# Feed-forward of a two-layer hybrid backbone: the down products of two inner blocks gather in PSUM before they are added to the running sum

## What is computed

```python
def swiglu(h, w1, w2):
    gate, up = jnp.split(h @ w1, 2, axis=-1)
    return (jax.nn.silu(gate) * up) @ w2
```

## Time and profile before

| | us |
|---|---|
| median of 3 runs | 4626.42 |
| lowest, highest | 4623.34, 4635.23 |
| the profiled execution | 4631.18 |
| its span | 4629.5 |
| TensorE busy with matmuls | 3859.6 (83%) |
| TensorE busy with weight loads | 3059.9 (66%) |
| VectorE busy | 2037.8 (44%) |
| ScalarE busy | 1087.3 (23%) |
| GpSimd busy | 492.6 (11%) |

### The profile page before, as it was taken

One profiled execution on the slowest core, in us unless ns is written; L12 is line 12 of the kernel. 1 busy time (PEld: TensorE's weight loads), 2 busy tenths in 40 slices (PEclk: granted clock), 3 DMA queues, 4 the chain that ended last, 5 costly groups with the idle time before them and its releaser, 6 DMA issues. The chain is left out here.

```text
span 4629.5 us, 55289 instructions
## 1 busy us (share of the span) xinstructions
PE 3859.6 (83%) x22802; PEld 3059.9 (66%) x22802; DVE 2037.8 (44%) x2175; ACT 1087.3 (23%) x1434; POOL 492.6 (11%) x314
## 2 busy tenths in 40 slices
PE   3998468939785999999996899469767859999996
PEld 2887336438674888888884788345356647777774
DVE  3111657645423343444345121667656234544445
ACT  1000332425314111111114000332345131111113
POOL 1000403002005000000003000511022040000000
PEclk6999679968897999999997999679889879999998
DMA  5222430041223101111105222240132211111111
GB/s 185 82 82 79 156 134 21 12 108 23 86 77 123 42 27 41 41 35 32 41 18 164 80 82 78 104 141 5 46 82 68 66 63 51 41 54 41 51 35 73
DMA packets 339917, 320.39 MB, mean 69 GB/s; under 512 B 42718, under 2 KB 310602, under 8 KB 339786
## 3 DMA queue, kind: packets, MB, share of 16 engines
q1 hardware_dynamic: 297514, 265.07, 18.5%
q0 software_dynamic: 6912, 31.46, 2.3%
q10 hardware_dynamic: 35360, 22.02, 1.5%
HBM read 248.17 MB, written 73.30 MB: 69 GB/s over the span
## 5 line engine op out<-in xcount | busy, mean ns | idle before, releaser
L477 PE MATMUL psum<-h_hi,f_whi 128*128 128x512 f32 (+1 forms) x1760 | 485.1, 373 | 70.7 <-DVE f_wlo L922 70.7
L927 DVE TENSOR_TENSOR y<-y,psum 128x1280 f32<-128x1280 f32 (+1 forms) x352 | 476.8, 1355 | 109.3 <-PE psum L477 103.9
L477 PE MATMUL psum<-h_lo,f_whi 128*128 128x512 f32 (+1 forms) x1760 | 481.6, 371 | 0.0
L477 PE MATMUL psum<-h_hi,f_wlo 128*128 128x512 f32 (+1 forms) x1760 | 481.4, 371 | 0.0
L477 PE MATMUL psum<-h_hi,w_hi 128*128 128x512 f32 x1472 | 379.2, 364 | 118.2 <-DVE w_lo L543 118.2
L477 PEld LDWEIGHTS psum<-h_hi,f_whi 128*128 128x128 f32 x1760 | 306.8, 188 | 135.0 <-DVE f_wlo L922 71.2
L477 PE MATMUL psum<-h_lo,w_hi 128*128 128x512 f32 x1472 | 377.4, 363 | 0.0
L477 PE MATMUL psum<-h_hi,w_lo 128*128 128x512 f32 x1472 | 377.0, 362 | 0.0
L922 DVE TENSOR_TENSOR f_wlo<-f_raw,f_whi 128x1024 fp32r<-128x1024 f32 x132 | 161.0, 1221 | 481.9 <-ACT f_whi L893 423.5
L477 PEld LDWEIGHTS psum<-h_hi,w_hi 128*128 128x128 f32 x1472 | 249.9, 190 | 164.3 <-issue 119.1
L893 ACT CAST f_whi<-f_raw 128x1024 fp32r<-128x1024 f32 x132 | 138.4, 1048 | 907.3 <-PE psum L477 882.5
(11 more groups left out here) (264 smaller groups left out, 5706.9 us busy)
## 6 DMA issues: line engine op xcount, KB each, us to landing
f_raw<-in_w_ffn_in SPq DMA_DIRECT2D x88, 512.0 KB, 6.0
proj_cm<-lin_stage POOLq DMA_DIRECT2D x48, 640.0 KB, 4.1
w_raw<-in_w_in SPq DMA_DIRECT2D x48, 512.0 KB, 5.0
ada_w<-in_w_ada SPq DMA_DIRECT2D x24, 1024.0 KB, 10.8
f_raw<-in_w_ffn_out SPq DMA_DIRECT2D x44, 512.0 KB, 3.6
ln_x<-x_cm SPq DMA_DIRECT2D x18, 1024.0 KB, 7.9
att_raw<-proj_cm SPq DMA_DIRECT2D x48, 320.0 KB, 5.7
x_cm<-ln_x SPq DMA_DIRECT2D x14, 1024.0 KB, 4.4
```

Source lines behind the costliest of these rows:

```text
L477: ins = nc.tensor.matmul(out[:, t0:t0 + tn], w, h[:, t0:t0 + tn], start=start and n == 0, stop=stop and n == 2)
L927: nc.vector.tensor_tensor(y[:, o, 0:tokens], y[:, o, 0:tokens], sets(o), ALU.add).then_inc(s_acc.h, 1)
```

## The change

Blocks j = 2p and 2p + 1 form pair p (HP = 11 pairs). The down product is made once per pair: for each of the eight outputs the matmuls of both blocks follow one another into the same PSUM set as one sum, and VectorE adds that to `y` once. The first pair's outputs are copied to `y` instead, and the memset on GpSimd is gone. The down weights of both blocks have to be there at once, so hi and lo of them get buffers of their own, `d_hi` and `d_lo`, two each. Outputs begin in set b. TensorE's order for a pair is gate product of 2p, down product of pair p - 1, up product of 2p, gate and up product of 2p + 1.

```diff
-        w_hi = k.sb(st, "f_whi", [P, 3, D], F32R)
-        w_lo = k.sb(st, "f_wlo", [P, 3, D], F32R)
+        w_hi = k.sb(st, "f_whi", [P, 2, D], F32R)
+        w_lo = k.sb(st, "f_wlo", [P, 2, D], F32R)
+        d_hi = k.sb(st, "f_dhi", [P, 2, D], F32R)
+        d_lo = k.sb(st, "f_dlo", [P, 2, D], F32R)
...
-            @block.gpsimd
-            def _(pool):
-                for j in range(KB):
-                    nc.gpsimd.memset(y[:, j, 0:tokens], 0.0).then_inc(k.sem("y_zero").h, 1)
...
                     act.wait_ge(s_h.h, s_h.at(1) + j)
-                    if not (isinstance(j, int) and j < 2):
-                        act.wait_ge(s_out.h, s_out.at(-KB) + j * KB)
+                    if not first:
+                        act.wait_ge(s_out.h, s_out.at(0) + p * KB)
                     nc.scalar.copy(u_hi[:, q, 0:tokens], hid[:, 0:tokens]).then_inc(s_uhi.h, 1)
-                    hi(2, j, first)
+                    act.wait_ge(s_w[2].h, s_w[2].at(16) + j * 16)
+                    nc.scalar.copy(d_hi[:, q], raw[:, 2]).then_inc(s_hi[2].h, 1)
...
-                def gather(j):
+                def gather(p, first=False):
                     for o in range(KB):
-                        dve.wait_ge(s_out.h, s_out.at(1 + o) + j * KB)
-                        nc.vector.tensor_tensor(y[:, o, 0:tokens], y[:, o, 0:tokens], sets(o), ALU.add).then_inc(s_acc.h, 1)
-
-                def block_j(j, q, more=True):
+                        dve.wait_ge(s_out.h, s_out.at(1 + o) + p * KB)
+                        if first:
+                            nc.vector.tensor_copy(y[:, o, 0:tokens], sets(o + 1)).then_inc(s_acc.h, 1)
+                        else:
+                            nc.vector.tensor_tensor(y[:, o, 0:tokens], y[:, o, 0:tokens], sets(o + 1), ALU.add).then_inc(s_acc.h, 1)
+
+                def block_j(j, q, before=None, first=False, more=True):
                     if more:
                         lo(0, j + 1)
+                    if before:
+                        before()
                     dve.wait_ge(s_silu.h, s_silu.at(1) + j)
...
                     nc.vector.tensor_tensor(hid[:, 0:tokens], act_g[:, 0:tokens], sets(1), ALU.mult).then_inc(s_h.h, 1)
-                    if not (isinstance(j, int) and j < 1):
-                        gather(j - 1)
...
-                dve.wait_ge(k.sem("y_zero").h, k.sem("y_zero").at(KB))
...
-                with dve.Fori(1, HB // 2 - 1) as i:
-                    for q in range(2):
-                        block_j(i * 2 + q, q)
-                block_j(HB - 2, 0)
+                block_j(2, 0, before=lambda: gather(0, True))
+                block_j(3, 1)
+                with dve.Fori(2, HP - 1) as p:
+                    block_j(p * 2, 0, before=lambda: gather(p - 1))
+                    block_j(p * 2 + 1, 1)
+                block_j(HB - 2, 0, before=lambda: gather(HP - 2))
                 block_j(HB - 1, 1, more=False)
-                gather(HB - 1)
+                gather(HP - 1)
...
-                def down(j, q, last=False):
-                    pe.wait_ge(s_lo[2].h, s_lo[2].at(1) + j)
-                    pe.wait_ge(s_ulo.h, s_ulo.at(1) + j)
+                def down(p, last=False):
+                    pe.wait_ge(s_lo[2].h, s_lo[2].at(2) + p * 2)
+                    pe.wait_ge(s_ulo.h, s_ulo.at(2) + p * 2)
                     for o in range(KB):
-                        if o == 0 and not last:
-                            pe.wait_ge(s_silu.h, s_silu.at(2) + j)
-                        elif o == 1 and not last:
-                            pe.wait_ge(s_h.h, s_h.at(2) + j)
+                        if o == 0:
+                            pe.wait_ge(s_h.h, s_h.at(2) + p * 2)
+                        elif o == 1:
+                            pe.wait_ge(s_silu.h, s_silu.at(2 if last else 3) + p * 2)
                         else:
-                            pe.wait_ge(s_acc.h, s_acc.at(o - 1) + j * KB)
+                            pe.wait_ge(s_acc.h, s_acc.at(o - 1) + p * KB)
                         cols = slice(o * P, (o + 1) * P)
-                        ins = three_products(nc, sets(o), chunks, w_hi[:, 2, cols], w_lo[:, 2, cols], u_hi[:, q], u_lo[:, q], True, True)
+                        for q in range(2):
+                            ins = three_products(nc, sets(o + 1), chunks, d_hi[:, q, cols], d_lo[:, q, cols], u_hi[:, q], u_lo[:, q], q == 0, q == 1)
                         ins.then_inc(s_out.h, 1)
...
+                def pair(p, first=False):
+                    if not first:
+                        pe.wait_ge(s_silu.h, s_silu.at(0) + p * 2)
+                    up(0, p * 2)
+                    if not first:
+                        down(p - 1)
+                        pe.wait_ge(s_acc.h, s_acc.at(-1) + p * KB)
+                    up(1, p * 2)
+                    if first:
+                        pe.wait_ge(s_silu.h, s_silu.at(1))
+                    else:
+                        pe.wait_ge(s_acc.h, s_acc.at(0) + p * KB)
+                    up(0, p * 2 + 1)
+                    pe.wait_ge(s_h.h, s_h.at(1) + p * 2)
+                    up(1, p * 2 + 1)
```

More of the change, by code:

```diff
@@ L844, in swiglu @@
     chunks = token_chunks(tokens)
+    HP = HB // 2
     w1 = k.a["w_ffn_in"][l].rearrange("(j p) n -> p j n", p=P)
@@ L858, in swiglu @@
         s_lo = [k.sem(f"{x}_lo") for x in kinds]
-        s_mm = [k.sem(f"{x}_products") for x in kinds]
+        s_mm = [k.sem(f"{x}_products") for x in kinds[:2]]
         s_silu, s_h, s_uhi, s_ulo, s_acc, s_out = (k.sem(x) for x in ("silu_done", "hidden_done", "hidden_hi", "hidden_lo", "acc_done", "down_out"))
@@ L888, in hi, with block_j @@
                     act.wait_ge(s_w[n].h, s_w[n].at(16) + j * 16)
-                    if not first and n < 2:
+                    if not first:
                         act.wait_ge(s_mm[n].h, s_mm[n].at(0) + j)
-                    elif not first:
-                        act.wait_ge(s_out.h, s_out.at(0) + j * KB)
                     nc.scalar.copy(w_hi[:, n], raw[:, n]).then_inc(s_hi[n].h, 1)
-                def block_j(j, q, first=False, more=True):
+                def block_j(j, p, q, first=False, more=True):
                     act.wait_ge(s_mm[0].h, s_mm[0].at(1) + j)
-                    if not first:
+                    if not (first and q == 0):
                         act.wait_ge(s_h.h, s_h.at(0) + j)
@@ L977, in down @@
                         ins.then_inc(s_out.h, 1)
-                def block_j(j, q):
-                    if isinstance(j, int) and j == 1:
-                        pe.wait_ge(s_silu.h, s_silu.at(1))
-                    if not (isinstance(j, int) and j < 2):
-                        pe.wait_ge(s_acc.h, s_acc.at(-2 * KB + KB - 1) + j * KB)
-                    up(0, j)
-                    if isinstance(j, int) and j == 1:
-                        pe.wait_ge(s_h.h, s_h.at(1))
-                    if not (isinstance(j, int) and j < 2):
-                        pe.wait_ge(s_acc.h, s_acc.at(-KB) + j * KB)
-                    up(1, j)
-                    if not (isinstance(j, int) and j < 1):
-                        down(j - 1, 1 - q)
@@ L992, in _ @@
-                block_j(0, 0)
-                block_j(1, 1)
-                with pe.Fori(1, HB // 2) as i:
-                    for q in range(2):
-                        block_j(i * 2 + q, q)
-                down(HB - 1, (HB - 1) % 2, last=True)
+                def pair(p, first=False):
+                    if not first:
+                        pe.wait_ge(s_silu.h, s_silu.at(0) + p * 2)
+                    up(0, p * 2)
+                    if not first:
+                        down(p - 1)
+                        pe.wait_ge(s_acc.h, s_acc.at(-1) + p * KB)
+                    up(1, p * 2)
+                    if first:
+                        pe.wait_ge(s_silu.h, s_silu.at(1))
+                    else:
[3 more added lines that the diff above has]
+                    up(1, p * 2 + 1)
@@ L998, in swiglu @@
+                pair(0, True)
+                pair(1)
+                with pe.Fori(2, HP) as p:
+                    pair(p)
+                down(HP - 1, last=True)
     for n in range(3):
+        for x in (s_hi, s_lo):
+            x[n].done(HB)
         s_w[n].done(16 * HB)
-        for x in (s_hi, s_lo, s_mm)[:3 if n < 2 else 2]:
-            x[n].done(HB)
-    for x in (s_silu, s_h, s_uhi, s_ulo):
+    for x in (s_silu, s_h, s_uhi, s_ulo, *s_mm):
         x.done(HB)
     for x in (s_acc, s_out):
-        x.done(HB * KB)
@@ L1006, in swiglu @@
-    k.sem("y_zero").done(KB)
+        x.done(HP * KB)
 def window_start(pair):
```

18 lines of the change are left out of this document (9 added, 9 removed).

## The result

| | before | after |
|---|---|---|
| median (4 runs each) | 4625.96 | 4595.27 |
| lowest, highest | 4623.34, 4635.23 | 4586.64, 4598.96 |
| the profiled execution | 4631.18 | 4598.96 |
| its span | 4629.5 | 4597.3 |
| feed-forward of layer 0, of layer 1 | 959.3, 763.5 | 946.9, 735.6 |

The changed kernel is faster: the ratio of the times is estimated at 0.9923, with a 95% interval of 0.9907 to 0.9939 (the two medians by themselves give 0.9934, 30.7 us). A feed-forward is counted here from its first weight load to the first load of the stage behind it. The two together went from 1722.8 to 1682.6, **40.2 us shorter**. The stages around them, whose code is the same, took 8.0 us more in this one execution.

The account below looks back on a forecast made before the run. The prediction took the hand-over of PSUM to the gather to bound the down products. Its terms, 36.2 + 5.3 - 2.8, gave 38.7 us faster, a median of 4588 us, range 4579 to 4603.

Parts of the forecast that it names:

- The busy row: TensorE reads busy for all of both steady feed-forward stretches, yet matmul start times show 0.43 and 1.255 us lost per block.
- Pairs, 36.2: Feed-forward down products: 18 matmuls per output release PSUM early, so the whole loss per block goes, 36.2 us gained.
- The hand-over of PSUM to the gather bounds the down products: Freeing a PSUM set takes 1.75 and 1.48 us, against 1.76 and 1.36 of matmuls per output in layers 0 and 1.
- 176 gathers fewer, worth nothing by themselves: On VectorE 238 us of work goes, but it lies beside the matmuls and gains nothing by itself.
- Copies and waits moved: The first pair's 16 copies out of PSUM and the down products' moved waits fit beside matmuls, at no cost.
- No memset, 5.3: At each feed-forward's start VectorE's first split no longer waits for GpSimd: 4.1 and 1.2 us earlier, 5.3 together.
- The tail, 2.8 lost: Before each layer's last down product the operand chain lies open; TensorE idles 5.6 and 4.8 us, 2.8 us lost together.
- clock 0: The slow clock after the idle stretch before the last down product stays as it is: 0, some 3 us in the range.
- A: Rival: TensorE is full and the loss per down product is something else that stays; no gain, 4624 us; chance 0.06.
- B: Rival: each PSUM hand-over costs its tenth of a microsecond however early; half of 36.2 goes, 4606 us; chance 0.08.
- C: Rival: the gather, behind the next gate weights' split and a late load, makes TensorE wait; slower, 4652 us; chance 0.03.

Follow-up runs that it names:

- order alone: Kernel before with each down product moved between gate and up product, one per block, gathers first on VectorE; one run, 4625.76 against 4627.37 us.

## Why the prediction was right

**The time.** 4588 was forecast (4579 to 4603); 4595.27 and 4590.76 were measured, 30.7 and 38.9 us under the kernel before. That a median comes so near is partly luck, with runs that differ by up to 20 us. The stages are the sounder test: the sum was 38.7 us and they gave 40.2; the first profile hid 8.0 of it in stages that the change doesn't touch. The 1.5 us beyond the sum are loads that landed sooner (1.0) and the clock (0.4), below.

**The busy row is no evidence.** Held: busy for all of 240 us before and after, and 3.9% more matmuls in the second case. The start times were the right view. The rule that heavier occupancy names the engine to work on (the Trainium skill, Perfetto Trace Analysis, Identifying the Most-Contended Engine) would have kept 2.5 us of the gain; 40.2 came, with VectorE busy for less than half of the stretch. The same page of the Trainium skill (Optimizing Tensor Performance, Matmuls) has it that matmul groups should rotate through PSUM banks so that one's evacuation overlaps the next one's matmuls. Two sets did rotate here; the rows add that the overlap is complete only where one output takes longer than 0.26 us plus the gather, by a margin: at 1.76 against 1.75 (layer 0, order alone) a down product still lost 0.26 us.

**Pairs, 36.2.** The size held: 33.7 from the periods, exactly. The attribution did not, in part. The step "The hand-over of PSUM to the gather bounds the down products" explains 0.26 of 0.43 and 1.00 of 1.255 in the order of the change. In the old order, where the other waits cover some of it, outputs 2 to 7 of layer 1 account for 0.56 of 1.255; the rest was the next product's wait for a gather (0.30) and output 1's wait for the hidden product (0.39), which the prediction had at nothing. I had seen that wait in the code, and wrote that it "lies beside" the matmuls now without asking what it had cost before. The sum was taken from the period, not from the loop, and so was right all the same: the order and the pairs take away both. Of the 33.7 us the order alone gave 8.4 in the periods, and the pairs on top of it 25.3; pairs in the old order were not run.

**176 gathers fewer, worth nothing by themselves.** Held in layer 0: with the reading work doubled again the pair took 84.50 as before.

**Copies and waits moved.** Held: copies of 1.22 and 1.49 us in the first pair, no period disturbed.

**No memset, 5.3.** Held: 4.1 of it in layer 0, where the first matmul is 2.36 us behind the cast instead of 6.44; 1.2 in layer 1, 2.36 instead of 3.59. Alone it gave 5.5 in the stages. In the profile of the change layer 1 gained a further 1.1 because its first load landed sooner (cast 3.83 us after the issue instead of 4.93), in the other direction 0.14 in layer 0. No step had that.

**The tail, 2.8 lost; clock 0.** The idle stretches came out at 5.59 and 4.84 for 5.6 and 4.8. But the time from the last silu to the end of the stage did not grow, and two terms explain it. The last two down products gave back the loss I had given three quarters of (0.65 and 1.9 us; not measured by itself, but with it the balance closes to 0.1 us in each layer). And the clock moved, in layer 0 for the better: 3.36 us at 0.50 instead of 5.47 at 0.51, worth 1.0; in layer 1 for the worse: 2.96 us at 0.50 and 2.00 at 0.65 against 2.25 at 0.50 and 2.00 at 0.77 before, worth 0.6. "The longer stretch leaves that as it is" was wrong for each layer, and came out within 0.4 us for the two together because they cancelled, which is luck.

**The rivals.** A is excluded by the periods, B by them and by the copies that cost nothing in time. C did not happen, yet it was nearer than its 0.03 says: its place is real (65.8 us slower without pairs), and it is missed by 0.75 us once per pair in layer 1; one copy more ahead of the gather was enough to bring its wait back. I had derived 16.0 us for the due time and 9.5 + L for the gather; what decided in the trace was not the load but silu, cast and split, which begin at the end of the gate product. Loads were early enough nearly always: behind the start of the stages ScalarE waited for one four times, all in layer 1, for 0.16 to 0.36 us, out of the 0.75 that are left; in the second profile of the change never.

## What to carry to other kernels

Where an engine reads as fully busy, measure the distance between the starts of equal units and compare it with the same unit where it waits for nothing; sum what is missing, and take the gain from that period. Then ask of each wait in the unit what it costs, one by one, since one edit can take away several and another edit only one of them. When accumulating longer in PSUM, the gain is that a unit becomes longer than the hand-over loop (here 0.26 us plus the reader's time), and a loop just as long as the unit still costs; moving other work ahead of the reader spends that very slack.

## What was not expected

- A first group of matmuls behind a wait that has only just ended takes about 0.11 us longer in starts (0.56 instead of 0.45 for two of 512 columns), even where the row shows no idle time.
- After idle stretches of 3.58 to 5.59 us the granted clock was near 0.50, but for 3.2 to 5.4 us with no order in it: the longer idle (5.59) had the shorter slow stretch (3.4) than the shorter one (4.12, then 5.4). An idle time of 1.95 was followed by full clock; one of 1.82 by 0.89 in the first microsecond and 0.50 in the next; 0.92 and 0.76 by none lower. What decides between them isn't shown by these runs.
- Stages with identical code took between 2894.8 and 2914.7 us in the twelve profiles, a scatter of 20 us. In one of them a group of four matmuls of a preparing stage takes 1.98 us at a granted clock of 1.00 in one profile of the change and 3.78 us at 0.50 in the other, so the clock granted to short bursts has a part in it; how much was not measured.
